# Softmax attention in a fused two-block model: both score pieces of a unit issued together, and keys and values of the differential heads loaded head by head

## The reference, cut to what matters

```
def sink_attention(qg, k, v, sink, valid):            # windowed heads: 8 queries, 2 keys/values
    s = einsum('bqhgd,bkhd->bhgqk', qg, k) * ATTN_SCALE
    s = where(valid, s, NEG_INF)                      # band of 3 x 128 keys, and 256 of the context
    p = softmax(concatenate([s, sink_col], -1), -1)[..., :-1]
    return einsum('bhgqk,bkhd->bqhgd', p, v)

def diff_attention(q1, q2, k1, k2, v, lam):           # differential heads: 4
    s1 = einsum('bqhd,bkhd->bhqk', q1, k1) * ATTN_SCALE
    s2 = einsum('bqhd,bkhd->bhqk', q2, k2) * ATTN_SCALE
    w = softmax(s1, -1) - lam * softmax(s2, -1)       # over all 1024 + 256 keys
    return einsum('bhqk,bkhe->bqhe', w, v)
```

## Time and profile before

| | us |
|---|---|
| median of 3 runs (lowest, highest) | 3732.4 (3731.8, 3734.17) |
| the profiled execution: its own time | 3732.36 |
| its span, first to last instruction | 3730.4 |
| context units of this stage | 543 to 590 |
| the 32 pairs | 590.6 to 1011, then the last turns to 1024 |
| mean granted TensorE clock over the span | 0.954 of 2.4 GHz |

### The profile page before, as it was taken

One profiled execution on the slowest core, in us unless ns is written; L12 is line 12 of the kernel. 1 busy time (PEld: TensorE's weight loads), 2 busy tenths in 40 slices (PEclk: granted clock), 3 DMA queues, 4 the chain that ended last, 5 costly groups with the idle time before them and its releaser, 6 DMA issues. The chain is left out here.

```text
span 3730.4 us, 52592 instructions
## 1 busy us (share of the span) xinstructions
PE 3377.7 (91%) x21774; PEld 2899.0 (78%) x21774; DVE 1628.8 (44%) x2517; ACT 1226.5 (33%) x2230; POOL 260.4 (7%) x332
## 2 busy tenths in 40 slices
PE   7899978999878999897999998887888899999998
PEld 2699976666667999875888995556766799999777
DVE  2306725555565112165526104553555455444343
ACT  3212325555564234124524103443332211111232
POOL 2000000000011000111211100001110000000010
PEclk9899989999988999998999998998998899999999
DMA  9224550000053222233321212001003111111332
GB/s 329 85 83 148 157 186 24 12 12 12 12 209 129 74 75 75 89 104 136 108 51 41 86 39 62 12 1 7 2 2 114 63 45 45 50 46 34 124 125 95
DMA packets 196721, 289.30 MB, mean 78 GB/s; under 512 B 41606, under 2 KB 137670, under 8 KB 194480
## 3 DMA queue, kind: packets, MB, share of 16 engines
q1 hardware_dynamic: 176624, 216.90, 18.0%
q0 software_dynamic: 19904, 69.65, 5.7%
HBM read 217.60 MB, written 68.90 MB: 77 GB/s over the span
## 5 line engine op out<-in xcount | busy, mean ns | idle before, releaser
L115 PE MATMUL p_pb<-p_w_hi,h_hi 128*128 128x416 f32 (+2 forms) x1216 | 424.7, 349 | 6.9 <-DVE p_w_lo L110 6.9
L117 PE MATMUL p_pb<-p_w_hi,h_lo 128*128 128x416 f32 (+2 forms) x1216 | 421.8, 347 | 0.0
L116 PE MATMUL p_pb<-p_w_lo,h_hi 128*128 128x416 f32 (+2 forms) x1216 | 419.6, 345 | 0.0
L115 PE MATMUL fu_pf<-h_hi,fu_w_hi 128*128 128x344 f32 (+1 forms) x1056 | 339.3, 321 | 8.7 <-DVE fu_pf L3422 8.7
L116 PE MATMUL fu_pf<-h_lo,fu_w_hi 128*128 128x344 f32 (+1 forms) x1056 | 340.2, 322 | 0.0
L117 PE MATMUL fu_pf<-h_hi,fu_w_lo 128*128 128x344 f32 (+1 forms) x1056 | 338.8, 321 | 0.0
L115 PEld LDWEIGHTS p_pb<-p_w_hi,h_hi 128*128 128x128 f32 x1216 | 229.0, 188 | 16.0 <-issue 14.6
L116 PEld LDWEIGHTS p_pb<-p_w_lo,h_hi 128*128 128x128 f32 x1216 | 229.2, 188 | 1.9
L117 PEld LDWEIGHTS p_pb<-p_w_hi,h_lo 128*128 128x128 f32 x1216 | 228.9, 188 | 0.7
L115 PEld LDWEIGHTS fu_pf<-h_hi,fu_w_hi 128*128 128x128 f32 x1056 | 199.7, 189 | 9.1 <-DVE fu_pf L3422 9.1
L117 PEld LDWEIGHTS fu_pf<-h_hi,fu_w_lo 128*128 128x128 f32 x1056 | 199.6, 189 | 0.0
(11 more groups left out here) (521 smaller groups left out, 7174.7 us busy)
## 6 DMA issues: line engine op xcount, KB each, us to landing
mod_w<-in_adaln_w SPq DMA_DIRECT2D x12, 2048.0 KB, 16.0
fu_raw<-in_ffn_up SPq DMA_DIRECT2D x88, 256.0 KB, 3.1
fd_raw<-in_ffn_down SPq DMA_DIRECT2D x44, 512.0 KB, 3.6
la_qkv<-p SPq DMA_DIRECT2D x16, 1024.0 KB, 5.0
p<-p_o SPq DMA_DIRECT2D x60, 208.0 KB, 1.9
s_raw<-in_w_in POOLq DMA_DIRECT2D x48, 256.0 KB, 3.5
rT<-p_stage SPq DMA_DIRECT2D x10, 896.0 KB, 4.8
p_raw<-in_ab_w_in POOLq DMA_DIRECT2D x10, 832.0 KB, 6.8
```

The lines of the kernel that those rows point to most:

```text
L115: pe.matmul(out, left[0], right[0], start=start, stop=False)
L116: pe.matmul(out, left[0], right[1], start=False, stop=False)
L117: return pe.matmul(out, left[1], right[0], start=False, stop=stop)
```

## The change

On TensorE, both pieces of a unit's scores are issued one after the other, and turn 0 of unit `u - 2` follows them; before, turn 0 stood between the two pieces. The wait for that unit's weights (`weighed`) moves with turn 0.

On SP, the load of `KB` is cut into four, one for each differential head, and so is that of `vb`, with a semaphore for each; they are issued head by head, with `va` behind the first head's. TensorE waits for a head's keys before that head's first score of tile 0, and for its values before the products of that unit.

```diff
-        keys_in, vb_in, ka_in, va_in, q0_in, q1_in = ph.sems("keys_in vb_in ka_in va_in q0_in q1_in")
+        ka_in, va_in, q0_in, q1_in = ph.sems("ka_in va_in q0_in q1_in")
+        keys_in = ph.sems("keys_in0 keys_in1 keys_in2 keys_in3")
+        vb_in = ph.sems("vb_in0 vb_in1 vb_in2 vb_in3")
...
-                sp.dma_start(KB[:, :, 0:SEQ], rT[KB_AT:KB_AT + 4, :, 0:SEQ].rearrange("c p t -> p c t")).then_inc(keys_in, 16)
-                sp.dma_start(vb[:, 0:NT, :], p0[0:SEQ, V_B:V_B + 512].rearrange("(t p) d -> p t d", p=P)).then_inc(vb_in, 16)
-                sp.dma_start(va[:, 1:1 + NT, :], p0[0:SEQ, 640:768].rearrange("(t p) d -> p t d", p=P)).then_inc(va_in, 16)
+                for j in range(4):
+                    sp.dma_start(KB[:, j, 0:SEQ], rT[KB_AT + j, :, 0:SEQ]).then_inc(keys_in[j], 16)
+                    sp.dma_start(vb[:, 0:NT, P * j:P * j + P], p0[0:SEQ, V_B + P * j:V_B + P * j + P].rearrange("(t p) d -> p t d", p=P)).then_inc(vb_in[j], 16)
+                    if j == 0:
+                        sp.dma_start(va[:, 1:1 + NT, :], p0[0:SEQ, 640:768].rearrange("(t p) d -> p t d", p=P)).then_inc(va_in, 16)
...
                     if u < NU:
                         if u == 6:
-                            pe.wait_ge(keys_in, 16)
                             pe.wait_ge(q0_in, 16)
+                        if units[u][0:2] == ("da", 0):
+                            pe.wait_ge(keys_in[units[u][2]], 16)
...
                         score(u, 0)
+                        score(u, 1)
                     if u >= 2:
                         weighed(u - 2)
                         turn(u - 2, 0)
-                    if u < NU:
-                        score(u, 1)
-                    if u >= 2:
-                        if u - 2 == 6:
-                            pe.wait_ge(vb_in, 16)
+                        if units[u - 2][0:2] == ("da", 0):
+                            pe.wait_ge(vb_in[units[u - 2][2]], 16)
                         if u - 2 == 7:
                             pe.wait_ge(va_in, 16)
                         turn(u - 2, 1)
```

## The result

The changed kernel is slower: ratio 1.0112, 95% interval 1.0081 to 1.0143 (median 3783.4 us, lowest 3765.7, highest 3789.6, against 3733.3, now of four runs, of which the fourth took 3747.5). Measured again in other rounds it is 1.0121 (1.0096 to 1.0147). The profiled execution took 3789.61 us, its span is 3787.7, so 57.3 us more than before; the medians lie 50 us apart. Two stages hold nearly all of the 57.3.

The account below looks back on a forecast made before the run. It took the attention stage as bound by a chain of scores, transposes, one-buffer evacuations and exponentials, no engine full. Span 3730.4 + 37.5 (score order) + 24 (clock) + 0.3 (waits) = 3792.2, plus 2.0: 3794.2 us; range 3758 to 3826.

Parts of the forecast that it names:

- Rival A: Attention pairs: the scores' end sets the exponentials, so earlier maxima make it 41 us faster, 3692 us; chance 0.06.
- Part 1, `da`: Joined scores in `da` units: turn 1 starts 3.69 us after the first score instead of 3.13, 0.56 later.
- The seam of 0.2: In `da`, time saved when nothing separates the score pieces: 0.2 us, taken between bounds 0 and 0.4.
- Part 1, `wa`: Joined scores in `wa` units: piece 1, formerly free during turn 0's evacuation, adds 0.65 us (0.45 to 0.75).
- the 14.2 to 14.4 that I gave as a sign: Attention stage: pairs of 14.2 to 14.4 us at full clock in the profile after would show the prediction right.
- Part 2, the clock: Attention pairs: longer stretches without scores drop TensorE's clock in about 17 pairs, 15 × 1.6 = 24 us more.
- the place grows: Stretch without scores grows to 5.1 us in `wa` and 4.9 in `da`, so more clock falls are expected.
- a granted clock below 0.98 in the stage: Attention stage: a sign, expected in the profile after, that the clock falls more often.
- The 24 us: Attention pairs: the cost of further clock falls, 15 × 1.6 us, between ends of 0 and 48 us.
- rival B: Attention stage: slower, but the clock holds, 3770 us; chance 0.30.
- Part 3, the loads: SP's queue before the attention stage: split loads cost 0 on the path, four issues 30 us at most, added waits 0.3.
- the 1 us that I had named as a sign: Start of attention stage: first matmul after the warm-up moving by more than 1 us would show the loads part wrong.

Follow-up runs that it names:

- e7: Kernel before, but in `wa` turn 0 goes ahead of both joined score pieces and turn 1 into a second buffer; median 3715.2 us, ratio 0.9939, pair 12.43 us.
- e8: Kernel before with only a second buffer for turn 1 in `wa`, scores still in two pieces; pair 12.87 us.
- r2_before_again: The kernel before, unchanged, profiled once more; attention stage 429.9 us, later softmax stage 259.8 us.
- e6: Kernel before, but in `wa` turn 0 is issued ahead of both joined score pieces, one buffer; pair 12.54 us, stage 415.1 us, its one execution 3736.95 us.
- e1: Kernel before with only the order of the scores changed (pieces joined), loads as before; median 3777.5 us, ratio 1.0104, pair 14.44 us.
- run 72: Not a run's label: "run" is a verb here, for the later softmax stage's 72 us at 1.2 GHz in executions where it took 280.8 us.
- r1: The changed kernel, unaltered, measured once more; median 3784.7 us against 3737.5 for the kernel before, attention stage 471.1 us.
- e2: Kernel before with only keys and values loaded head by head, scores in the old order; ratio 1.0002, pair 13.09 us.

## Why the prediction was right or wrong

**The bound.** Right. ScalarE's 0.0 us ahead of its exponentials stayed 0.0, and the maxima, 0.78 us earlier, found nobody waiting. Rival A needed ScalarE to wait on VectorE; that came only in `e7` and `e8`, after the evacuations' chain was made shorter.

**Part 1, `da`.** Right to the hundredth: turn 1 at 3.69, +0.56. The seam of 0.2, a guess between two bounds, was right too (joined scores take 2.35).

**Part 1, `wa`.** The mechanism was right and the term too small: +0.79 instead of 0.65, near the far bound of 0.75 and past it. The pieces: the context matmuls start 1.39 us after the first score (I had 1.30), turn 0 follows 0.64 later, and its evacuation starts 0.69 after it, where I had kept the 0.63 of the earlier trace rows. So a pair came to 14.44, just above the 14.2 to 14.4 that I gave as a sign. A pair costs 1.35 instead of 1.21, 31 pairs 41.9 instead of 37.5. The stage grew by 37.7 in the two profiles and by 40.9 against `r2_before_again`: the first profile of before had two slow pairs (14.68 us) and a fall behind the last pair, the one after has one slow pair (16.13), `r2_before_again` has none. Without the slow pairs the growth is 39.2. What is missing from 41.9 is mostly the end: from the last pair's first score to the last store it took 24.27 us and now takes 22.77, 1.5 less, which I hadn't counted.

The Trainium skill's "Perfetto Trace Analysis", Matmuls (under Optimizing Tensor Performance), wants independent groups in different PSUM banks, so that the evacuation of one overlaps the matmuls of the next; the runs agree, the second buffer gave back 1.26 us a pair where the cover was gone. The Trainium skill's "Perfetto Trace Analysis", Matmul Optimizations, wants matmuls back to back in batches. The joined scores did save 0.2 us of TensorE's time (2.35 against 2.55), but the pair became 1.35 us longer and the clock in the pairs was hardly different, so here that rule followed by itself cost time. With turn 0 ahead of them (`e6`), joined scores in `wa` went with a pair 0.55 us shorter than before.

**Part 2, the clock.** Wrong. The place of the falls was read rightly: both begin 0.2 us after the first score of a `da`, behind the end of `wa` without scores, and so does the one after the change.

```profile
core 0: us, PE busy (x) PEld busy (x) DVE busy (x) ACT busy (x) POOL busy (x), PEclk, DMA share, GB/s
800.00:803.40 3.40, 3.40 (x10) 1.45 (x12) 0.18 (x1) 0.52 (x1) 0.00 (x0) 0.50 0.00 0
919.50:922.80 3.30, 3.30 (x10) 1.33 (x10) 0.10 (x1) 0.53 (x1) 0.00 (x0) 0.50 0.40 159
```
```profile
919.26 1.07 PE L1057 MATMUL att_pS<-att_KB,att_qT 64*128 64x512 f32 x2 [0.74 <-ACT att_E L916]
```
```profile
935.60:938.90 3.30, 3.30 (x10) 1.28 (x10) 0.00 (x0) 0.00 (x0) 0.00 (x0) 0.50 0.00 0
```
```profile
935.33 1.07 PE L1061 MATMUL att_pS<-att_KB,att_qT 64*128 64x512 f32 x2 [0.74 <-ACT att_E L920]
```

In the twelve profiles there are seven such falls between the first pair's scores and the last pair's, and all seven begin 0.1 to 0.2 us after a `da`'s first score. The failed step is the one from there to "So more falls are to be expected", with "the place grows" for its reason. The place did grow, as I had worked out: TensorE has no scores for 5.15 us in `wa` (814.72 to 819.87) and for 4.91 in `da` (807.78 to 812.69). The falls did not: one in the pairs of the changed kernel, in either of its profiles, at most one in each of the eight experiments `e1` to `e8`, whether a pair took 12.4 or 14.4 us, and none in the second profile of the kernel before. Two events in 32 pairs carried the term, and I took the middle between two ends for want of a row. The sign that I had given, a granted clock below 0.98 in the stage, didn't come either; it was 1.00. The 24 us measured 1.5 us the other way: one slow pair of 1.7 us where there had been two of 1.6.

**The total.** The number came out near by luck. In place of the 24 us stand the 20.9 us of the later stage, which I hadn't considered. So the forecast of 3794.2 lies 4.6 us above the profiled execution and 10.8 above the median, but the part that the runs show to be the change's is the 38 to 41 us of its own stage, which is rival B (3770): that was the right case. The medians lie 50 us apart, in the later round 47, in `e1` 43; the intervals of all three ratios hold 41 us. What makes the later stage run 72 us at 1.2 GHz in one execution and 14 in another is open. So is whether the changed kernel meets it more often: with 41 us taken off, six of its ten timed executions took 3743 us or more, and of the kernel before 13 of 41. Two smaller things: the upper end of the range adds up to 3827, not 3826, and a measurement couldn't tell 0.2% from no change here, since executions of the kernel before alone differ by 0.7%.

**Part 3, the loads.** Right: 0 on the path. The price was less than my bound: SP's queue was free at 551.8, 2 us later than before, not 30, and the queries landed 16.3 us after their issue, at 565.5, 24 us ahead of the first pair. The first pair's score moved by 0.6 us here, but by 2.2 in `r1` and 3.1 in `e2`, both times to the earlier side and with less time at 1.2 GHz in the context units (26.1 and 22.5 us against 31.7); so the 1 us that I had named as a sign against this part was no good sign.

```profile
548.76 0.44 SPq L885 DMA_DIRECT2D att_vb<-p  x1
549.24 2.51 SPq L888 DMA_DIRECT2D att_qT<-rT  x1
```

The load of 512-byte rows that held SP for 7.48 us before and 7.49 after is `va`; the four `vb` loads of the same form and size held it 0.44 to 1.97 us. So the length of an issue wasn't the price of that form. My guess is that it depends on what stands in the queue before it; no run shows that.

## What to carry to other kernels

Work that stands between two steps of a chain may be what covers the chain's other half. Before it is moved together with its like, ask what runs on the other engine while it runs, and whether the chain ever waits for its result; here nothing on the chain waited for the scores, and ScalarE waited for the transposes in every round. Where one buffer makes two engines alternate, give it a second one or issue its first step into a wait that exists anyway. Against the kernel before, the second buffer was worth 0.22 us a pair here, the first step in the wait 0.55, both together 0.66.

## What the runs showed of the hardware

Executions of one and the same kernel differ by up to 28 us (the kernel before: 3726.4 to 3754.0 over 13 executions). Two profiles of the changed kernel differ by 24 us in one stage, which runs tens of us at 1.2 or at 2.4 GHz (257.1 and 280.8 us for the same instructions). For a change of 1% the length of its own stage in the profile is the sharper measure: with joined scores it repeats within 0.6 us (470.8, 470.5, 471.1), and in the kernel before the 3.2 us between 433.1 and 429.9 are the two slow pairs. Sharper still is the median pair, the same to the hundredth in each repetition (13.09, 14.44).

TensorE's clock fell in a stretch in which it never stood idle for more than 0.8 us at a time: in seven places of twelve profiles, each time 0.1 to 0.2 us after the first score that follows 3.8 to 5.2 us of transposes, narrow products and a wait. The same stretch passed without a fall in all other pairs, so it doesn't make the fall by itself.

Two pieces of scores of the same shape cost 0.2 us less when nothing stands between them (2.35 us against 1.06 + 1.49).
